# The four slots of the split weights start 64 bytes further on, every other buffer keeps its place modulo 256 bytes

## The reference

```
f = swiglu(rms_norm(h, ln_ffn1[i, 0]), ffn1_w_gu[i], ffn1_w_down[i])
h = h + 0.5 * rms_norm(f, ln_ffn1[i, 1])
...
m = short_conv_mixer(hn, ...)      # layer 0;  diff_attention_mixer(hn, ...) in layer 1
h = h + rms_norm(m, ln_mix[i, 1])
...
a = jnp.square(jax.nn.relu(nm @ w_ff1))
h = h + a @ w_ff2
```

## The kernel before

| products | columns | offset before |
|---|---|---|
| gu0 to dn2, conv, values and keys of the heads (L1956 to L1958 and the opening blocks) | 272 | 192 |
| query part of the heads (`part(i, 1)`) | 256 | 0 |
| attn_out, gu3, dn3, mix_in, mix_out, ff1 | 256 | 32 |
| ff2 | 512 | 224 |
| `keep_warm`, an activation by itself (L2126) | 272 or 256 | 0 |

## Time and profile before

### The profile page before, as it was taken

The page is one execution under the profiler, slowest core; times in us unless marked ns, Lnnn a source line. Parts: engine busy times, 40 slices in busy tenths (PEclk is TensorE's granted clock), DMA queues, the critical chain, the costliest instruction groups (busy, mean ns, idle before and its releaser), DMA issues.

```text
span 1344.7 us, 26044 instructions
## 1 busy us (share of the span) xinstructions
PE 1332.8 (99%) x10628; PEld 1289.8 (96%) x10628; DVE 895.8 (67%) x1364; ACT 660.2 (49%) x957; POOL 12.2 (1%) x26
## 2 busy tenths in 40 slices
PE   9999999999999999999999999999999999999998
PEld 9999999999999999999999999999999999999886
DVE  6666548768666548666548997866655867777444
ACT  5443535446444535444545666644444545644333
POOL 0000000000000000000000000000001000000000
PEclk9999999999999999999999999999999999999999
DMA  8555553444555533555552323455655523555551
GB/s 294 185 186 199 209 187 140 143 134 149 188 173 208 204 134 125 189 167 212 200 200 108 126 95 126 153 187 190 215 211 199 177 91 117 178 182 186 172 187 60
DMA packets 29884, 228.16 MB, mean 170 GB/s; under 512 B 3472, under 2 KB 3920, under 8 KB 6000
## 3 DMA queue, kind: packets, MB, share of 16 engines
q1 hardware_dynamic: 28656, 224.27, 47.6%
q0 software_dynamic: 864, 2.35, 0.5%
q10 hardware_dynamic: 288, 0.48, 0.1%
HBM read 226.01 MB, written 1.06 MB: 169 GB/s over the span
## 4 chain that ended last, share of the span: by engine, by line
PE 91%; DVE 6%; ACT 2%; issue 1%; DVEq 0%; POOL 0%; ACTq 0%; POOLq 0%
PE ps L1956 23%; PE ps L1957 23%; PE ps L1958 23%; PE ps L2625 2%; PE ps L2624 2%; PE ps L2623 2%; PE ps L1998 1%; PE ps L2038 1%; PE ps L1993 1%; PE ps L1994 1%; PE ps L2026 1%; ACT w_hi L581 1%; PE ps L2279 1%; DVE w_lo L1125 1%; PE ps L2004 1%
## 5 line engine op out<-in xcount | busy, mean ns | idle before, releaser
L581 ACT ACTIVATE w_hi<-w_raw 128x2048 fp32r<-128x2048 f32 (+2 forms) x175 | 373.9, 2136 | 367.3 <-PE ps L1958 301.2
L1125 DVE TENSOR_TENSOR w_lo<-w_raw,w_hi 128x2048 fp32r<-128x2048 f32 (+2 forms) x163 | 413.1, 2535 | 211.4 <-ACT w_hi L581 211.4
L1956 PE MATMUL ps<-x_hi,w_hi 128*128 128x272 f32 (+1 forms) x1920 | 548.8, 286 | 0.2 <-DVE hid L1856 0.2
L1957 PE MATMUL ps<-x_lo,w_hi 128*128 128x272 f32 (+1 forms) x1920 | 544.9, 284 | 0.0
L1958 PE MATMUL ps<-x_hi,w_lo 128*128 128x272 f32 (+1 forms) x1920 | 544.8, 284 | 0.0
L1956 PEld LDWEIGHTS ps<-x_hi,w_hi 128*128 128x128 f32 x1920 | 361.5, 188 | 5.3 <-issue 3.5
L1957 PEld LDWEIGHTS ps<-x_lo,w_hi 128*128 128x128 f32 x1920 | 361.6, 188 | 0.1
L1958 PEld LDWEIGHTS ps<-x_hi,w_lo 128*128 128x128 f32 x1920 | 361.5, 188 | 0.0
L1956 PE MATMUL ps<-hid_hi,w_hi 128*128 128x272 f32 (+1 forms) x704 | 200.8, 285 | 0.3 <-DVE w_lo L1125 0.3
L1958 PE MATMUL ps<-hid_hi,w_lo 128*128 128x272 f32 (+1 forms) x704 | 200.4, 285 | 0.0
L1957 PE MATMUL ps<-hid_lo,w_hi 128*128 128x272 f32 (+1 forms) x704 | 200.4, 285 | 0.0
(11 more groups left out here) (350 smaller groups left out, 1691.9 us busy)
## 6 DMA issues: line engine op xcount, KB each, us to landing
w_raw<-w_gu SPq DMA_DIRECT2D x86, 1024.0 KB, 4.9
w_raw<-w_dn SPq DMA_DIRECT2D x32, 1408.0 KB, 5.8
w_raw<-w_ff SPq DMA_DIRECT2D x32, 1024.0 KB, 5.0
w_raw<-w_conv_in SPq DMA_DIRECT2D x8, 1536.0 KB, 6.2
w_raw<-w_qkv SPq DMA_DIRECT2D x8, 1536.0 KB, 6.4
w_raw<-w_mix_in SPq DMA_DIRECT2D x8, 1536.0 KB, 6.3
w_raw<-w_conv_out SPq DMA_DIRECT2D x4, 1024.0 KB, 4.9
w_raw<-w_attn_out SPq DMA_DIRECT2D x4, 1024.0 KB, 4.9
```

The source lines that it names most:

```text
L581: act.activation(w_hi[j % SPLIT][:, 0:width], w_raw[j][:, 0:width], ACT.Copy).then_inc(hi_ready, 1)
L1125: dve.tensor_tensor(w_lo[j % SPLIT][:, 0:width], w_raw[j][:, 0:width], w_hi[j % SPLIT][:, 0:width].bitcast(F32), ALU.subtract).then_inc(lo ...
L1956: pe.matmul(out_ap, w_hi[slot][:, cols], hi(k), start=first, stop=False)
L1957: pe.matmul(out_ap, w_hi[slot][:, cols], lo(k), start=False, stop=False)
```

## The change

A filler of 16 elements (64 bytes) is allotted ahead of the split weights and one of 48 elements (192 bytes) behind them. The two fillers are never read or written. `w_hi` and `w_lo` start 64 bytes further on. All that is allotted behind them starts 256 bytes further on, at the same place modulo 256. `w_raw` does not move. No instruction, wait, order or size changes.

```
         w_raw = [sb(f"w_raw{i}", [P, SLOT]) for i in range(RAW)]
+        sb("before_weights", [P, 16])
         w_hi = [sb(f"w_hi{i}", [P, SLOT], F32R) for i in range(SPLIT)]
         w_lo = [sb(f"w_lo{i}", [P, SLOT], F32R) for i in range(SPLIT)]
+        sb("behind_weights", [P, 48])
         x_hi = sb("x_hi", [P, KD * X_ROW], F32R)
```

## The result

| | before | after |
|---|---|---|
| median of the executions | 1344.92 us (1344.68 to 1345.51, 4) | 1365.14 us (1365.07 to 1366.13, 4) |
| profiled execution, its span | 1346.38 us, 1344.7 us | 1365.14 us, 1363.4 us |
| predicted | | 1364 us, range 1344 to 1370 |

The ratio is 1.0149, 95% interval 1.0136 to 1.0161. The change costs 20.2 us by the medians, 18.7 us from span to span.

A forecast was written before the change was run, and what follows sets the result against it. TensorE's pitch between matmul starts was taken as the bound. 5946 272-column matmuls at 3.33 ns (+19.8 us) and the query part (-0.6 us) gave 1345.06 + 19.2 = 1364.3, rounded to 1364 us; range 1344 to 1370.

The forecast's parts named there:

- 272-column products at offset 128: 5946 matmuls going from offset 192 to 128 take the longer pitch, 3.33 ns each: +19.8 us.
- Nothing on VectorE and ScalarE: Splits of the weights on these engines: taken as 0, with a bound of some 50 ns on 2048 elements.
- ff2 unchanged: 512-column products of ff2, offset 224 to 32: taken as 0, pitch stays at 233.3 ns.
- my case of no change: Rival for the whole kernel: operand reads do not meet at 128, 272 columns stay at 123.3 ns, 1345 us; chance 0.15.
- the step: Inference from L2279's 191 ns weight loads at offset 128 to 272 columns: gu2 loads 192 ns, pitch about 126.7.
- The change exchanges the two. I take 0.: 256-column products go from offset 32 to 224 and ff2 from 224 to 32; both claimed harmless, 0 us.
- The bound that I gave: For 256-column products and ff2: the step between the two pitches seen, 3.3 ns on each.
- The rival that these products take the longer pitch: About 3,300 256-column products by 3.3 ns add 11 us, about 1376 us; 0.10, shared with a price above 3.5 ns.
- the query part: Heads' 192 matmuls of 256 columns leave offset 0 for 192: 120.0 to 116.7 ns, -0.6 us.
- the sum of 19.2 us: Whole kernel: +19.8 us for 272-column products and -0.6 us for the query part.

The follow-up runs named there:

- e1: Kernel before with the 64-byte filler ahead of the weights and none behind, so weights and activations move together at unchanged offsets; 1345.6 us, ratio 0.9999.
- e2: Kernel before with weights unmoved and all behind them moved back 64 bytes modulo 256, giving the changed kernel's offsets; 1365.67 us, ratio 1.0145.
- e3: Kernel before with the weights moved by 128 bytes, 272 columns at offset 64; 1364.80 us, ratio 1.0141.
- e4: Kernel before with the weights moved by 32 bytes, 272 columns at offset 160, 256 columns and ff2 at 0; 1351.76 us, ratio 1.0042.
- e8: Kernel before with the weights moved by 224 bytes, 272 columns at offset 224, gu3 and ff1 at 64; 1358.37 us, ratio 1.0090.
- e7: Kernel before with the weights moved by 192 bytes, 272 columns at offset 0, 256 columns at 96; 1365.26 us, ratio 1.0141.
- e10: Kernel before with ff2's hidden activation written 56 elements further on in `hid_hi` and `hid_lo`, ff2 at offset 0; 1343.48 us, ratio 0.9987.
- e9: Kernel before with 64 bytes between `w_hi` and `w_lo`, so only `w_lo` moves; 1363.76 us, ratio 1.0135.
- e11: Kernel before with ff1's activation begun 8 elements further on in `x_hi` and `x_lo`, ff1 at offset 64; 1345.44 us, ratio 0.9994.
- e12: Kernel before with both ff2's hidden activation moved to offset 0 and ff1's activation to offset 64; 1343.15 us, ratio 0.9984.

## Why the prediction came out right, point by point

**Right, as measured.** The bound: TensorE's pitch. The place: 272-column products at offset 128. The size of the step: 3.3 ns was forecast and 3.3 ns measured (123.3 to 126.7), with the steps of 272 columns that are ordinary in both traces adding 18.9 us where 19.8 were forecast. Nothing on VectorE and ScalarE, and ff2 unchanged. e1 and e2 show that the distance between the operands is what matters. The Trainium skill, "SBUF — State Buffer", sections on the two separate sides of SBUF and on who interferes with whom, has TensorE never wait on anyone, which was my case of no change. The trace does not agree: 126.7 ns against 123.3, by the layout alone.

**Right number, wrong reason.** I carried a weight load of 191 ns from 128-column plain float32 at offset 128 over to 272 columns, and expected loads of 192 ns in gu2. I had written that 188 ns there would refute the step. They are 188 ns. The longer pitch at 128 does not show in the recorded load. I had concluded from 0 and 128 that the pattern repeats every 128 bytes; e3 refuted that (126.7 ns at 64, 123.3 at 192). The forecast held because 272 columns are slow at six of the eight offsets that were tried, which my rows could not tell me.

**Mis-sized: the 256-column products.** "The change exchanges the two. I take 0." That step failed. At 224 they have 118.3 ns, 1.67 ns more, on about 3,300 products 5.5 us; the 3183 steps outside the heads that are ordinary in both traces add 4.7 us. The bound that I gave (3.3 ns) held it. The argument was that 512 columns at 224 show no slow load. Width counts too, and e4 to e8 show that one width tells little of another. The rival that these products take the longer pitch was half right, at half its price. Its aside that the load covers less than half of the pitch at 512 columns does not fit the rows: 188 ns of 233.3 are 81%.

**Right way, wrong pitch: the query part.** 116.7 ns was forecast; six of seven rows have 113.3 and one 117.7. Over the 160 steps that are ordinary in both traces it is -0.8 us, against -0.6 forecast.

**Missing: what is given back.** Ordinary steps add 18.9 + 4.0 = 22.9 us, and the time grew by 20.2 us by the medians. The difference, 2.7 us, is in the long steps, of which the border above is one. That the other engines catch up there was argued from the order of the work and not tried by an experiment. I had treated all of TensorE's standing time as fixed. The other moves show the same when their steps are paired with those of before in the same way: e4's ordinary steps give 7.6 us and it lost 6.3 us (1351.76 - 1345.46), e7's give 22.1 and it lost 18.9 (1365.26 - 1346.38), e8's give 15.7 and it lost 12.0 (1358.37 - 1346.38). Four executions of before stand behind the 1346.38 and spread over 1.7 us, so the last two losses are rough. So of the sum of 19.2 us the 272 columns were 0.9 too high, the 256 columns outside the heads 4.7 too low and the waits, put at nothing, 2.7 too high: the errors nearly met, which is luck, and 1364 was closer than its working deserved.

**Expectations behind the result.** e1, e2 and the ff2 part of e10 came as expected, the rest in part or not. e9 was the clearest miss, and e11 fell because ff1's 113.3 ns in e8 did not follow its offset alone.

**Open.** What in the chip joins the two addresses was not shown. The runs tell neither whether the moving read or the weight load waits, nor why three products in a row settle on one total. That a settled pitch changes only at a pause was seen; why ff1 then stands at 113.3, 116.7 or 117.8 ns, and at 117.8 after a change that did not touch it, stays open too. The measured times of e11 fall into two groups, 1342.95 to 1344.14 us and 1345.44 to 1347.13, and those of e12 into three. That looks like pitches chosen anew in each execution, but a profile covers one execution of each kernel, and no run here decides it.

## What to carry to other kernels

Where back-to-back float32r matmuls set the time, the start of the moving operand less that of the stationary one, modulo 256 bytes, is a parameter of the kernel. It was worth up to 1.5% here, so any change that shifts a buffer should be timed against one in which a filler keeps the distance. The 256 rest on this kernel's rows of 1280 bytes and tiles of 512: inside one product the distance moves by odd multiples of 256, and the pitch stays. Measure it per width on the kernel's own products: an offset that is good for one width told nothing of another, and one pitch seen at an offset is not yet the pitch of that offset. When the busiest engine gets slower, expect some of the sum of its steps to be given back where short waits for other engines shrink. In the changed kernel it was 2.7 of 22.9 us, 12%. Before such a share is read from two traces, compare their granted clocks, which here made up a third of the apparent 4.1 us.

## What the hardware showed that I had not expected

- The pitch takes few values at each width: 123.3, 125.3, 125.7 and 126.7 ns with 272 columns, 113.3, 116.7, 117.4, 117.8, 118.3, 118.7 and 120.0 with 256, 226.7, 228.9, 233.3 and 234.3 with 512. At 2.4 GHz (granted clock 1.00) 113.3, 116.7 and 120.0 ns are 272, 280 and 288 cycles, 123.3 and 126.7 are 296 and 304, and 226.7 and 233.3 are 544 and 560: multiples of 8. The values between them are not.
- The fastest pitch, 113.3 ns, is 272 cycles for 256 columns. The 272-column products never came closer to their own column count than 296 cycles.
- The weight load is recorded with 188 or 192 ns. 192 goes with 120.0 ns at 256 columns and offset 0 (e4, and the earlier trace rows), but a pitch that is longer by the same 3.3 ns at 272 columns shows 188 (gu2 after the change), and so do 120.0 ns at 256 columns and offset 96 (e7).
- Moving one of two weight buffers by 64 bytes costs as much as moving both (1.0135 against 1.0149), and changes the steps of the products that did not move.
- The same products at the same offset can run at two pitches in one execution, and the change from one to the other comes at a pause: ff1 of e8 has 117.8 ns ahead of a step of 0.19 us and 113.3 behind it.
